# The second block's attention in head pairs, with its input normalised once and its work shifted between engines

## The chip, the cores and the metric

The kernel runs on one core of a Trainium2 chip. A core has TensorE (PE, matmuls), VectorE (DVE), ScalarE (ACT), GpSimd (POOL) and SyncE (SP), which here only issues the loads. Each engine runs its own instructions in the order written and waits on semaphores for the others. The metric is device time in microseconds (us) of one launch; lower is better.

## What is computed

A transformer block (`first_block`) and then a second one on 512 tokens of width 1024. The change lies in the second block, cut here to what matters:

```python
def second_block(x, mem, ...):
    h = rms_norm(x, norm_mix)
    q_a, k_a, v_a, u_b, gate_b, gate_c, g_a, g_b = jnp.split(h @ w_in, split_points, axis=-1)
    o_a = stick_breaking_attention(heads(q_a), heads(k_a), heads(v_a))   # 8 heads of 64
    y_b = gate_b * causal_depthwise_conv(gate_c * u_b, conv_w)           # 3 taps, 512 channels
    merged = sigmoid(g_a) * (o_a @ w_branch_a) + sigmoid(g_b) * (y_b @ w_branch_b)
    x = x + merged @ w_mix_out
    x = x + memory_cross_attention(rms_norm(x, ..), rms_norm(mem, ..), ...)
    ...
def stick_breaking_attention(q, k, v):      # per block of 128 queries, keys up to its end
    z = (q . k) * 64 ** -0.5
    log_fail = where(mask, log_sigmoid(-z), 0)          # mask: key < query
    log_later = reverse_cumsum(log_fail) - log_fail
    weights = where(mask, exp(log_sigmoid(z) + log_later), 0)
    return weights @ v
```

The input x of the second block is itself the output of a normalisation (the first block's last line), so two normalisations follow one another.

## The kernel before

Activations lie feature by token: `X[:, k, :]` is features 128k to 128k+127 of all 512 tokens. Every fp32 operand of a matmul is split into a high part (fp32r, rounded) and a low part (the rest), and each product is made of three matmuls: high by high, high by low, low by high. Weights come in units of 128 output features (128x1024, 512 KB): the load into `RAW`, ACT's copy to `WH` (helper `hi`, L1267), then the difference `WL` (helper `lo`, L1683). `WH` and `WL` have three slots (`NW`). The units `qb`, `kb` and `ub` (four each, 12 in all) have their `WL` made by POOL (L1647, `ON_POOL`), all others by DVE.

The program is one list of steps, written by the class `Order` and run through by every engine, each taking from it what is its own. A unit's matmuls (`gemm`: 24 of 128x512 into one of the two banks `G`) are emitted in two halves of 12, and each half begins with a `tick`. A step of attention is put some ticks ahead with `later(n, ...)`; steps put without it follow at once. So the list sets what stands between two halves on PE, and in what order DVE and ACT come to their work.

`block_b` is the part changed. It runs so:
- `v_gemm("vb", ...)`: the values of all heads, 96 matmuls into the banks `SC` and `TP`, from `XGh`, `XGl`, which hold x times its gain, not yet normalised. Within it `norm2` makes both row scales on DVE and ACT: `RB1` for the first block's final norm, then `RB` for the second block's, each with an Ln, an Exp and three steps on DVE (`refine`), and at last `RB` times `RB1` (L1768).
- For each head pair p the units `qb`, `kb`, `ub`, `gc`, `gb`. As `XG` isn't normalised, each result is multiplied by `RB` when it leaves PSUM: `qk_b` on DVE (L2005), then ACT's high and DVE's low part; `conv_u` on DVE, a product on POOL in `conv_g` (L1667), one more product in `taps`.
- The attention, head by head, four steps each (i, the block of 128 queries; keys 128(i+1)). `scores_b`: three matmuls of 64 rows into one of three banks (`score_bank`), then DVE adds the mask to the last 128 columns (L2050). `weights_b`: ACT's sigmoid of -z and of z (L1540, L1543), DVE's reverse running product (L2058) and the product of both (L2061). `turn_b`: PE transposes the weights by 128x128 (L1143), ACT and DVE make the two parts `WTh`, `WTl`. `pv_b`: 12 matmuls with the values into `O`. ACT and DVE take it out.
- The gates `sa`, `sb`: DVE multiplies by `RB` (`gate_b`, L2078), ACT takes the sigmoid (L1556, `sigmoid_b`), then the branches `bb`, `ba` are multiplied in (`branch`, L2085) and summed.

The first block's attention (`scores_a` and what follows it) already takes its two score maps of a head in the two halves of the rows, in alternation, six matmuls a step.

Of the kernel before, what the change touches and what calls it, by code (L numbers as in the profile page):

```python
# [11 lines left out]
ALU = mybir.AluOpType  # L12
ACT = mybir.ActivationFunctionType
# [30 lines left out]
ON_POOL = ("qb", "kb", "ub")  # L44
# [15 lines left out]
STAGES_A = (("exp_a", 1), ("weights_a", 2), ("turn_a", 4), ("wt_a", 5))  # L60
CLOSING_A = (("pv_a", 6), ("sq_a", 7), ("ss_a", 8), ("rs_a", 8), ("op_a", 9))
# [46 lines left out]
class Order:  # L108
# [80 lines left out]
    def gemm(self, name, i, step):  # L189
# [3 lines left out]
        late = wide and name in ("q", "k", "pool", "g0", "g1")  # L193
# [191 lines left out]

    def block_b(self):
        self.v_gemm("vb", 0, 4, {(0, 3): [("norm2",)], (3, 1): [("cols", "mix")]})
        for m in range(4):
            self.put("vev", "vb", 0, m)
        for k in range(8):  # L390
            self.later(2 + k, "scale_x", k)
        self.put("mask_b")
        for p in range(4):
            for w in range(2):
                self.gemm(("qb", "kb")[w], p, ("qk_b", p, w))
                self.put("qk_b", p, w)
            for j in range(8):
                h, i = 2 * p + j // 4, j % 4
                o = 1 + i + 5 * (j // 4)
                self.later(o, "scores_b", h, i)  # L400
                self.later(o + 1, "weights_b", h, i)
# [4 lines left out]
            self.put("conv_u", p)  # L406
            self.gemm("gc", p, ("conv_g", p))
            self.put("conv_g", p)
            self.later(1, "taps", p)
            self.gemm("gb", p, ("conv_y", p))  # L410
            self.put("conv_y", p)
            self.later(0, "conv_split", p)

        def gates(n):
            for w in range(2):
                self.gemm(("sa", "sb")[w], n, ("gate_b", n, w))
                self.put("gate_b", n, w)
                if n > 0:
                    self.put("sigmoid_b", n, w)

        def branch(n, w):
            self.gemm(("ba", "bb")[w], n, ("branch", n, w))
            if n == 0 and w == 1:
                self.put("sigmoid_b", 0, 0)
                self.put("sigmoid_b", 0, 1)
# [139 lines left out]
def program(nc, a, out):  # L565
# [5 lines left out]
    with ctx:  # L571
# [91 lines left out]
        def score_bank(s, n):  # L663
            return (SC[:, 0, 0:n], SC[:, 1, 0:n], M[:, 0:n])[s % 3]
# [24 lines left out]
        for v, (name, _, _) in enumerate(units):  # L689
# [6 lines left out]
        EMPTY = tally("qk", "residual", "up", "qk_b", "conv_u", "conv_g", "conv_y", "gate_b",  # L696
                      "branch", "km", "qm", "fg", "fu", "res_half")
# [3 lines left out]
        MOVED = tally("gate", "pool_in")  # L701
# [8 lines left out]

        NRM, n = {}, 0
        for step in steps:
            if step[0] in ("norm", "norm2", "norm_half"):
                n += 1 + (step[0] == "norm2")
                NRM[step] = n
# [32 lines left out]
        TURN = tally("turn_a", "turn_b")  # L748
# [1526 lines left out]
```

## Time and profile before

| | us |
|---|---|
| median of three runs | 1639.52 |
| lowest, highest | 1635.52, 1639.94 |
| the profiled execution, its time | 1636.55 |
| its span, first to last instruction | 1634.8 |
| PE busy | 1596.5 (98%) |
| DVE busy | 927.3 (57%) |
| ACT busy | 629.5 (39%) |
| POOL busy | 117.0 (7%) |

The span has 7352 matmuls. The second block's `vb` begins near 727 us of the span, its attention runs from 768 to about 946, the gates go on to about 1045. A busy PE in this profile includes the tail of each pipelined matmul (a 128x512 one is shown with 0.39 us, but the next starts 0.227 us later), so idle time of PE and the distance between starts say more than its share of busy time.

### The profile page before, as it was taken

The numbers are of one execution on the slowest core, as the hardware profiler recorded it, in microseconds if no ns is written. First come the engines' busy times: TensorE is split into PE (matmuls) and PEld (weight loads), VectorE is DVE, ScalarE is ACT, GpSimd is POOL, SyncE is SP. The second block draws the span as 40 slices with busy tenths as digits, with TensorE's granted clock in tenths as the row PEclk, the third lists the DMA queues.
The fourth block names the chain that finished last, engine by engine and source line by source line (L and its number), as shares of the span: only waits on it lengthen the run. The fifth ranks groups of instructions, "written<-read, shape, count | busy, mean of one in ns | idle before, by whom it ended". The sixth has DMA issues, their size and how long they took to land.

```text
span 1634.8 us, 19078 instructions
## 1 busy us (share of the span) xinstructions
PE 1596.5 (98%) x7352; PEld 1303.1 (80%) x7352; DVE 927.3 (57%) x1380; ACT 629.5 (39%) x1008; POOL 117.0 (7%) x82
## 2 busy tenths in 40 slices
PE   8999989999999999999999999999999999999997
PEld 6777767788888888887777787789888888888886
DVE  6767666756644545356777645555555544434435
ACT  5355665743322222263344334335444332222213
POOL 3000000010000000042221010010002000000002
PEclk9999999999999999999999999999999999999999
DMA  5243222243333323222211132335222323232322
GB/s 198 80 117 101 77 75 66 68 155 96 98 103 91 103 91 103 91 91 91 66 64 59 55 119 78 115 95 178 65 90 91 103 91 99 95 103 90 102 85 72
DMA packets 49674, 155.64 MB, mean 95 GB/s; under 512 B 6192, under 2 KB 9136, under 8 KB 49456
## 3 DMA queue, kind: packets, MB, share of 16 engines
q1 hardware_dynamic: 49584, 154.42, 30.5%
q8 instruction: 59, 0.97, 0.3%
q14 instruction: 31, 0.25, 0.1%
HBM read 148.11 MB, written 2.10 MB: 92 GB/s over the span
## 4 chain that ended last, share of the span: by engine, by line
PE 88%; DVE 6%; ACT 3%; issue 2%; DMA 0%; DVEq 0%; SPq 0%; ACTq 0%
PE G L872 77%; PE SC L872 4%; PE O L872 2%; PE TP L872 2%; DVE WL L1683 1%; PE M L872 1%; PE TP L1143 1%; ACT WH L1267 1%; DVE XGl L1684 1%; PE M L1163 0%; ACT XGh L1267 0%; ACT X L1267 0%; DVE X L2189 0%; DVE X L1971 0%; ACT T L1454 0%
## 5 line engine op out<-in xcount | busy, mean ns | idle before, releaser
L872 PE MATMUL G<-XGh,WH 128*128 128x512 f32 x1248 | 502.0, 402 | 3.1 <-DVE Vl L1684 2.2
L872 PE MATMUL G<-XGh,WL 128*128 128x512 f32 x1248 | 488.9, 392 | 0.0
L872 PE MATMUL G<-XGl,WH 128*128 128x512 f32 x1248 | 488.9, 392 | 0.0
L1683 DVE TENSOR_TENSOR WL<-RAW,WH 128x1024 fp32r<-128x1024 f32 (+3 forms) x269 | 324.0, 1205 | 143.8 <-ACT WH L1267 143.3
L1267 ACT ACTIVATE WH<-RAW 128x1024 fp32r<-128x1024 f32 (+3 forms) x281 | 283.3, 1010 | 179.6 <-PE G L872 168.7
L872 PEld LDWEIGHTS G<-XGh,WH 128*128 128x128 f32 x1248 | 235.6, 189 | 65.2 <-issue 9.3
L872 PEld LDWEIGHTS G<-XGh,WL 128*128 128x128 f32 x1248 | 235.6, 189 | 50.6
L872 PEld LDWEIGHTS G<-XGl,WH 128*128 128x128 f32 x1248 | 235.7, 189 | 48.2 <-issue 2.2
L872 PE MATMUL G<-MGh,WH 128*128 128x512 f32 x412 | 161.1, 391 | 1.8 <-DVE F L2078 1.1
L872 PE MATMUL G<-MGl,WH 128*128 128x512 f32 x412 | 160.5, 390 | 0.2 <-DVE MGl L1683 0.2
L872 PE MATMUL G<-MGh,WL 128*128 128x512 f32 x412 | 160.4, 389 | 0.0
L1971 DVE TENSOR_TENSOR X<-X,G 128x512 f32<-128x512 f32 x76 | 52.1, 686 | 142.6 <-PE G L872 142.5
L1655 POOL TENSOR_TENSOR F<-F 128x512 f32<-128x512 f32 x34 | 48.6, 1429 | 758.7 <-ACT F L1339 757.9
L872 PEld LDWEIGHTS G<-MGh,WH 128*128 128x128 f32 x412 | 77.3, 188 | 19.6 <-DVE F L2078 1.8
L872 PEld LDWEIGHTS G<-MGl,WH 128*128 128x128 f32 x412 | 77.4, 188 | 16.2 <-DVE MGl L1683 0.5
L872 PEld LDWEIGHTS G<-MGh,WL 128*128 128x128 f32 x412 | 77.3, 188 | 16.2
L872 PE MATMUL G<-Vl,WH 128*128 128x512 f32 x224 | 87.2, 389 | 0.0
L872 PE MATMUL G<-Vh,WH 128*128 128x512 f32 x224 | 87.2, 389 | 0.0
L872 PE MATMUL G<-Vh,WL 128*128 128x512 f32 x224 | 87.2, 389 | 0.0
L1267 ACT ACTIVATE MGh<-T 128x512 fp32r<-128x512 f32 x38 | 24.0, 632 | 143.3 <-DVE T L2170 63.0
L1683 DVE TENSOR_TENSOR WTl<-TP,WTh 128x128 fp32r<-128x128 f32 (+1 forms) x64 | 31.1, 486 | 57.0 <-ACT WTh L1267 56.8
L1267 ACT ACTIVATE Vh<-T 128x512 fp32r<-128x512 f32 x24 | 15.2, 632 | 101.5 <-DVE T L1984 63.7
(310 smaller groups left out, 1873.3 us busy)
## 6 DMA issues: line engine op xcount, KB each, us to landing
RAW<-in_up SPq DMA_DIRECT2D x32, 512.0 KB, 3.6
RAW<-in_dn SPq DMA_DIRECT2D x32, 512.0 KB, 3.6
RAW<-in_fg SPq DMA_DIRECT2D x22, 512.0 KB, 3.6
RAW<-in_fu SPq DMA_DIRECT2D x22, 512.0 KB, 3.6
RAW<-in_g SPq DMA_DIRECT2D x16, 512.0 KB, 3.6
RAW<-in_f SPq DMA_DIRECT2D x16, 512.0 KB, 3.5
X<-in_x SPq DMA_DIRECT2D x16, 256.0 KB, 4.6
RAW<-in_q SPq DMA_DIRECT2D x8, 512.0 KB, 3.6
```

Of the source, the lines that this page charges most:

```text
L872: return e.matmul(dst, st, mv, start=start, stop=stop, skip_group_check=True)
L1143: t = e.transpose(TP[:, i % 2, j * P:(j + 1) * P], src[:, j * P:(j + 1) * P], ID[:, :])
L1267: return e.activation(dst, src, ACT.Copy, scale=scale)
L1655: e.tensor_tensor(acc, acc, sqs[arg[1] % 2], ALU.add).then_inc(acc_done, 1)
L1683: return e.tensor_tensor(dst, src, hi.bitcast(F32), ALU.subtract)
L1684: return e.scalar_tensor_tensor(dst, src, scale, hi.bitcast(F32), ALU.mult, ALU.subtract)
L1971: e.tensor_tensor(X[:, n, :], X[:, n, :], G[:, turn_of[step] % 2, :], ALU.add).then_inc(g_empty, 1)
```

## The change

- **Normalised once.** `xsplit 2` now writes `MGh`, `MGl` (x times gain, for `vb` alone). `norm2` makes only the combined scale `RB`, from both sums at once; eight new steps `xn_mul` and `xn_lo` write `XGh`, `XGl` from `F = X * gain * RB`, between the matmuls of `vb`. `RB1` is made later (`norm2b`). The products with `RB` behind each matmul fall away: `qk_b` is ACT's high part and DVE's low part straight from PSUM, `conv_u` is a copy on ACT, the gates are one sigmoid on ACT from PSUM (`sigmoid_b` is gone), POOL's product in `conv_g` and the last one of `taps` are gone.
- **Heads in pairs.** A step of the attention is now (p, i): the scores of both heads of pair p, six matmuls in alternation between rows 0 to 63 (into `SC` bank 0) and rows 64 to 127 (bank 1). Mask, sigmoids and the product of the weights take both heads in one instruction of double width; running products, transposes and value matmuls stay one per head. The second head's turned weights lie in `QK[:, :, 4:8, :]`, its output in bank `M`.
- **Ticks.** `attention_b` places the 16 steps 2.5 ticks apart, and the parts of each at 0 (`scores_b`), 1 (`fail_b`), 2 (`weights_b`), 4 (`turn_b`), 5 (`wt_b`), then 6 (`pv_b`) and 7 (`out_b`). What leaves `G` follows one tick later instead of at once. For `qb` to `gb` and the gates one weight split moves to the second half (`late`).
- **POOL.** `ON_POOL` is empty: the 12 splits go to DVE.

```diff
-ON_POOL = ("qb", "kb", "ub")
+ON_POOL = ()
+STAGES_B = (("fail_b", 1), ("weights_b", 2), ("turn_b", 4), ("wt_b", 5))
+CLOSING_B = (("pv_b", 6), ("out_b", 7))
+PACE_B = 2.5
...
-        late = wide and name in ("q", "k", "pool", "g0", "g1")
+        late = wide and name in ("q", "k", "pool", "g0", "g1", "qb", "kb", "ub", "gc", "gb", "sa", "sb")
...
+    def attention_b(self, start):
+
+        for s in range(16):
+            p, i = s // 4, s % 4
+            o = start + int(s * PACE_B) - self.clock
+            self.later(o, "scores_b", p, i)
+            for kind, n in STAGES_B:
+                self.later(o + n, kind, p, i)
+            if i == 3:
+                for kind, n in CLOSING_B:
+                    self.later(o + n, kind, p)
+
     def block_b(self):
-        self.v_gemm("vb", 0, 4, {(0, 3): [("norm2",)], (3, 1): [("cols", "mix")]})
+        between = {(0, 3): [("norm2",)]}
+        for k in range(9):
+            at = between.setdefault((1 + k // 4, k % 4), [])
+            if k < 8:
+                at.append(("xn_mul", k))
+            if k > 0:
+                at.append(("xn_lo", k - 1))
+        between[2, 3].append(("cols", "mix"))
+        self.v_gemm("vb", 0, 4, between)
...
+        self.later(4, "norm2b")
         for k in range(8):
-            self.later(2 + k, "scale_x", k)
+            self.later(8 + 3 * k, "scale_x", k)
         self.put("mask_b")
         for p in range(4):
             for w in range(2):
                 self.gemm(("qb", "kb")[w], p, ("qk_b", p, w))
-                self.put("qk_b", p, w)
-            for j in range(8):
-                h, i = 2 * p + j // 4, j % 4
-                o = 1 + i + 5 * (j // 4)
-                self.later(o, "scores_b", h, i)
-                self.later(o + 1, "weights_b", h, i)
-                self.later(o + 3, "turn_b", h, i)
-                if i == 3:
-                    self.later(o + 6, "pv_b", h)
+                self.later(0, "qk_b", p, w)
+            if p == 0:
+                self.attention_b(self.clock + 2)
...
PE, scores_b
+                    for part in range(3):
+                        for c in range(2):
+                            r = slice(c * HEAD, (c + 1) * HEAD)
+                            q, k = ((QKh, QKh), (QKh, QKl), (QKl, QKh))[part]
+                            if part == 0 and s == 0:
+                                e.wait_ge(v_lo, VEV["vev", "vb", 0, c])
+                            elif part == 0:
+                                e.wait_ge(sb_win, s)
+                            t = mm(SC[:, c, 0:n], q[r, sq_, qs], k[r, sk_, 0:n], start=(part == 0), stop=(part == 2))
+                            if part == 2:
+                                t.then_inc(sb_done, 1)
...
ACT, fail_b
+                    e.wait_ge(sb_masked, s + 1)
+                    e.activation(T[:, 4:6, 0:n], SC[:, :, 0:n], ACT.Sigmoid, scale=-1.0).then_inc(sb_fail, 1)
+                    if s >= 2:
+                        e.wait_ge(tb_done, 2 * s - 2)
+                    e.activation(weight_pair(s, n), SC[:, :, 0:n], ACT.Sigmoid).then_inc(sb_win, 1)
...
ACT, gate_b
+                    e.wait_ge(unit_done, gemm_done(step))
+                    e.activation(sgb[n % 2][w], G[:, turn_of[step] % 2, :], ACT.Sigmoid).then_inc(g_moved, 1)
...
DVE, xn_mul and xn_lo
+                    e.scalar_tensor_tensor(F[:, k % 2, :], X[:, k, :], gain(G_MIX, k), RB[:, :], ALU.mult,
+                                           ALU.mult).then_inc(xn_mul, 1)
+                    lo(XGl[:, k, :], F[:, k % 2, :], XGh[:, k, :]).then_inc(xn_lo, 1)
```

How the order moves, at three places. First PE, where the second head pair's first scores stand (`M` and `SC` are score banks, `TP` takes transposes, `G` the units' results). Before:

```order
L872 MATMUL G<-XGh,WL 128x512
L1143 MATMUL TP<-ID,T 128x128 x3
L872 MATMUL M<-QK 128x128 x3
L872 MATMUL G<-XGh,WH 128x512
L872 MATMUL G<-XGl,WH 128x512
```

And in the changed kernel:

```order
L891 MATMUL G<-XGh,WH 128x512
L891 MATMUL G<-XGl,WH 128x512
L891 MATMUL G<-XGh,WL 128x512
L891 MATMUL SC<-QK 128x128 x6
L891 MATMUL G<-XGh,WH 128x512
L891 MATMUL G<-XGl,WH 128x512
```

Three matmuls of one head have become six of two heads. They stood one half of `ub` (12 matmuls) behind the unit `kb` whose result they read; they stand a whole `ub` (24) behind it now.

Second DVE, from the first step of `norm2` on, within `vb` (`WL` is the split of its last unit). Before:

```order
L1757 TENSOR_SCALAR T<-M 128x512
L1692 TENSOR_TENSOR T<-F 128x512
L1694 SCALAR_TENSOR_TENSOR T<-T 128x512
L1696 SCALAR_TENSOR_TENSOR F<-T,F 128x512
L1760 TENSOR_TENSOR T<-F 128x512
L1763 SCALAR_TENSOR_TENSOR T<-O,T 128x512
L1765 TENSOR_SCALAR T<-T 128x512
L1692 TENSOR_TENSOR T<-RB 128x512
L1694 SCALAR_TENSOR_TENSOR T<-T 128x512
L1696 SCALAR_TENSOR_TENSOR RB<-T,RB 128x512
L1768 TENSOR_TENSOR RB<-RB,F 128x512
L1683 TENSOR_TENSOR WL<-RAW,WH 128x1024
```

And in the changed kernel:

```order
L1826 TENSOR_SCALAR T<-M 128x512
L1829 SCALAR_TENSOR_TENSOR T<-O,T 128x512
L1748 TENSOR_TENSOR T<-RB 128x512
L1750 SCALAR_TENSOR_TENSOR T<-T 128x512
L1752 SCALAR_TENSOR_TENSOR RB<-T,RB 128x512
L1739 TENSOR_TENSOR WL<-RAW,WH 128x1024
L1799 SCALAR_TENSOR_TENSOR F<-X,GN,RB 128x512 x2
L1739 TENSOR_TENSOR XGl<-F,XGh 128x512
```

Eleven instructions ahead of the split have become five, and behind it now come the 16 that write the normalised input.

Third DVE in the midst of the attention, at the scores of 384 and 512 keys. Before (third head):

```order
L2058 SCALAR_TENSOR_TENSOR T<-T 128x384
L2061 TENSOR_TENSOR T<-T 128x383
L2050 TENSOR_TENSOR SC<-SC,MSK 128x128
L2005 SCALAR_TENSOR_TENSOR T<-G,RB 128x512
L1683 TENSOR_TENSOR QK<-T,QK 128x512
L1683 TENSOR_TENSOR MGl<-O,MGh 64x512
L1683 TENSOR_TENSOR WTl<-TP,WTh 128x2x128
L2058 SCALAR_TENSOR_TENSOR T<-T 128x512
L2061 TENSOR_TENSOR T<-T 128x511
L1683 TENSOR_TENSOR WL<-RAW,WH 128x1024
```

And in the changed kernel (second pair):

```order
L2113 SCALAR_TENSOR_TENSOR T<-T 128x384 x2
L2116 TENSOR_TENSOR T<-T 128x2x383
L2104 TENSOR_TENSOR SC<-SC,MSK 128x2x128
L1739 TENSOR_TENSOR WL<-RAW,WH 128x1024
L1739 TENSOR_TENSOR QK<-G,QK 128x512
L2113 SCALAR_TENSOR_TENSOR T<-T 128x512 x2
L2116 TENSOR_TENSOR T<-T 128x2x511
L1739 TENSOR_TENSOR WL<-RAW,WH 128x1024
```

The running products come in twos, mask and product at double width; the split that POOL made stands among them, and the step that scaled a result by `RB` ahead of its split is gone.

## Rows read from the trace of the kernel before

**Rows 1.** The page: busy time of each engine and its share

```profile
PE 1596.5 (98%) x7352; PEld 1303.1 (80%) x7352; DVE 927.3 (57%) x1380; ACT 629.5 (39%) x1008; POOL 117.0 (7%) x82
```

**Rows 2.** Windows: from:to, length, PE, PEld, DVE, ACT, POOL busy, clock, DMA share, GB/s

```profile
768.00:931.00 163.00, 159.16 (x734) 123.14 (x734) 116.00 (x188) 64.01 (x134) 27.69 (x13) 1.00 0.20 60
934.00:937.00 3.00, 2.69 (x12) 2.26 (x13) 3.00 (x6) 1.46 (x3) 0.00 (x0) 0.78 0.13 36
937.00:940.00 3.00, 3.00 (x10) 2.38 (x9) 0.56 (x1) 0.00 (x0) 0.00 (x0) 0.65 0.57 181
```

**Rows 3.** Waits of PE, 727 to 1030 us: us in total, times, longest

```profile
PE TP L1143 <- DVE T L2061: 2.7, 1, 2.7
PE SC L872 <- DVE QK L1683: 2.6, 2, 1.3
PE SC L872 <- DVE WL L1683: 2.0, 1, 2.0
PE M L872 <- DVE QK L1683: 1.3, 1, 1.3
PE G L872 <- DVE F L2078: 1.1, 1, 1.1
```

**Rows 4.** Timeline of PE, first head: start, us, what; six rows

```profile
767.82 0.39 PE L872 MATMUL G<-XGh,WL 128*128 128x512 f32 x1
768.14 0.55 PE L872 MATMUL SC<-QK 64*128 64x128 f32 x3
768.62 0.50 PE L872 MATMUL G<-XGh,WH 128*128 128x512 f32 x1
...
771.55 0.61 PE L872 MATMUL SC<-QK 64*128 64x256 f32 x3
...
775.04 0.78 PE L872 MATMUL M<-QK 64*128 64x384 f32 x3
...
778.81 0.97 PE L872 MATMUL SC<-QK 64*128 64x512 f32 x3
```

**Rows 5.** Timeline of PE, the first block's attention, score steps

```profile
102.44 0.55 PE L872 MATMUL SC<-QK 64*128 64x128 f32 x6
...
112.12 0.79 PE L872 MATMUL SC<-QK 64*128 64x384 f32 x6
...
118.88 0.96 PE L872 MATMUL SC<-QK 64*128 64x512 f32 x6
```

**Rows 6.** Timeline of PE, scores that begin a head pair, with the idle time before

```profile
807.60 0.52 PE L872 MATMUL M<-QK 64*128 64x128 f32 x3 [1.26 <-DVE QK L1683]
...
849.30 0.52 PE L872 MATMUL SC<-QK 64*128 64x128 f32 x3 [1.29 <-DVE QK L1683]
```

**Rows 7.** Timeline of DVE in `norm2`, within `vb`

```profile
734.48 0.68 DVE L1757 TENSOR_SCALAR T<-M 128x512 f32<-128x512 f32 x1
...
744.19 2.77 DVE L1768 TENSOR_TENSOR RB<-RB,F 128x512 f32<-128x512 f32 x1
746.88 1.21 DVE L1683 TENSOR_TENSOR WL<-RAW,WH 128x1024 fp32r<-128x1024 f32 x1
```

**Rows 8.** Groups by form, DVE, 20 to 60 us: xcount, busy us, mean ns, idle

```profile
L1729 DVE SCALAR_TENSOR_TENSOR X<-X,GN,RB 128x512 f32<-128x512 f32 x8 | 5.9, 746 | 0.0
```

**Rows 9.** Groups by form, DVE, 734 to 1045 us

```profile
L1683 DVE TENSOR_TENSOR WL<-RAW,WH 128x1024 fp32r<-128x1024 f32 x26 | 31.7, 1219 | 8.7 <-ACT WH L1267 8.7
L2058 DVE TENSOR_TENSOR_SCAN T<-T 128x512 f32<-128x512 f32 x8 | 11.0, 1370 | 0.0
...
L2005 DVE SCALAR_TENSOR_TENSOR T<-G,RB 128x512 f32<-128x512 f32 x8 | 5.5, 683 | 5.1 <-PE G L872 5.1
```

**Rows 10.** Timeline of POOL, then of DVE, one moment near 773 us

```profile
772.85 2.62 POOL L1647 TENSOR_TENSOR WL<-RAW,WH 128x1024 fp32r<-128x1024 f32 x1 [14.10 <-ACT WH L1267]
...
773.32 2.30 DVE L2061 TENSOR_TENSOR T<-T 128x127 f32<-128x127 f32 x1
```

**Rows 11.** Groups by form, ACT, 734 to 1045 us

```profile
L1540 ACT ACTIVATE T<-SC 128x512 f32<-128x512 f32 x6 | 3.5, 590 | 1.1 <-DVE SC L2050 1.1
```

More of the change, by code:

```diff
@@ L714, in program @@
                 n += 1 + (step[0] == "norm2")
-                NRM[step] = n
+                SUM[step] = n
         ln_done, r_sq = sem("ln_done"), sem("r_sq")
@@ new lines, in _ @@
+                    for part in range(3):
+                        for c in range(2):
+                            r = slice(c * HEAD, (c + 1) * HEAD)
[7 more added lines that the diff above has]
+                                t.then_inc(sb_done, 1)
+                elif kind == "turn_b":
+                    p, i = arg
+                    s, n = 4 * p + i, (i + 1) * P
+                    e.wait_ge(wb_done, s + 1)
+                    for c in range(2):
+                        if s == 0:
+                            e.wait_ge(v_lo, VEV["vev", "vb", 0, 2 + c])
+                        else:
+                            e.wait_ge(wtb_lo, 2 * s - 1 + c)
+                        for j in range(i + 1):
+                            t = e.transpose(TP[:, c, j * P:(j + 1) * P], weight_pair(s, n)[:, c, j * P:(j + 1) * P],
+                                            ID[:, :])
+                        t.then_inc(tb_done, 1)
+                elif kind == "pv_b":
+                    p = arg[0]
+                    for c, bank in enumerate((O, M)):
+                        if p > 0:
+                            e.wait_ge(ob_lo, 2 * p - 1 + c)
+                        elif c == 0:
+                            e.wait_ge(v_lo, VEV["vev", "vb", 0, 3])
+                            e.wait_ge(ms_done, NRM["norm2",])
+                        else:
+                            e.wait_ge(col_done, COL["cols", "mix"])
+                        e.wait_ge(wtb_lo, 8 * p + 7 + c)
+                        pv_heads(bank, turned_of(c), lambda j: j, p).then_inc(pvb_done, 1)
@@ new lines, in _ @@
+                    if s >= 2:
+                        e.wait_ge(tb_done, 2 * s - 2)
+                    e.activation(weight_pair(s, n), SC[:, :, 0:n], ACT.Sigmoid).then_inc(sb_win, 1)
+                elif kind == "wt_b":
+                    p, i = arg
+                    s, n = 4 * p + i, i + 1
+                    for c in range(2):
+                        if i == 0 and p > 0:
+                            e.wait_ge(pvb_done, 2 * p - 1 + c)
+                        e.wait_ge(tb_done, 2 * s + 1 + c)
+                        v = TP[:, c, 0:n * P].rearrange("p (j q) -> p j q", q=P)
+                        hi(turned_of(c)[0][:, 0:n, i * P:(i + 1) * P], v).then_inc(wtb_hi, 1)
+                elif kind == "out_b":
+                    p = arg[0]
+                    for c, bank in enumerate((O, M)):
+                        r = slice(c * HEAD, (c + 1) * HEAD)
+                        e.wait_ge(pvb_done, 2 * p + 1 + c)
+                        hi(MGh[r, p, :], bank[r, :]).then_inc(ob_hi, 1)
+                elif kind == "gate_b":
@@ L2057, in _ @@
+                    W_, fail = weight_pair(s, n), T[:, 4:6, 0:n]
                     e.wait_ge(sb_fail, s + 1)
-                    e.tensor_tensor_scan(back, back, back, 1.0, ALU.mult, ALU.min).then_inc(wb_all, 1)
-                    e.wait_ge(wb_all, s + 1)
+                    for c in range(2):
+                        back = T[:, 4 + c, 0:n][:, ::-1]
+                        e.tensor_tensor_scan(back, back, back, 1.0, ALU.mult, ALU.min).then_inc(wb_all, 1)
+                    e.wait_ge(wb_all, 2 * s + 2)
```

331 lines of the change are left out of this document (148 added, 183 removed).

## The prediction

> **What bounds the kernel now.** I read the page first: TensorE is busy for 98% of the span, VectorE for 57%, ScalarE for 39%, GpSimd for 7% [rows 1]. So the kernel is as long as PE's list, and a change pays only by shortening that list or by taking away an idle moment of PE. The windows say the same of the part that is changed: from 768 to 931 us PE is busy 159.2 of 163 us and DVE 116.0 [rows 2]. Then the waits of PE from 727 to 1030 us, which name each idle moment: 2.7 us for the last head's weights, 2.6 and 1.3 us for a split of q or k, 2.0 us for a weight split within `vb`, 1.1 us for a result that a gate had not yet freed, 9.7 us in all [rows 3]; two more of 0.4 us I leave out of account. Last the timeline of PE itself, for what its list costs between two units.
>
> **The scores in pairs.** In the second block one head's step is three matmuls of 64 rows. They take 0.55, 0.61, 0.78 and 0.97 us for the four key lengths, and the next unit's first matmul starts 0.07 us before such a row ends (768.14 plus 0.55, against 768.62) [rows 4]. That is 2.91 less 4 times 0.07, or 2.63 us a head. Each visit also costs at its edges: 768.14 comes 0.32 us after the last matmul of the unit instead of 0.227, and the first one behind lasts 0.50 instead of 0.39 us [rows 4], 0.2 us a visit, 0.8 a head. One head's scores: 3.4 us. In the first block, where a step holds six matmuls in alternation between the two halves of the rows, it takes 0.55, 0.79 and 0.96 us at three of these lengths [rows 5], the same for twice the work. The change makes 16 steps of six out of 32 of three, with the same shapes, so four heads' worth goes: 4 times 3.4 = **13.7 us**. Transposes (80) and value matmuls (96) stay as many and as long, 0.
>
> **The waits for q and k.** Each head pair's first scores come 12 matmuls behind `kb`, and its result goes DVE, ACT, DVE; PE idles 1.26 and 1.29 us for it [rows 6], three times in all, 3.9 us by rows 3. Now ACT reads PSUM at once, DVE follows, and 24 matmuls (5.4 us) lie between. One result's path is then some 0.63 and 0.69 us: it fits four times. **3.9 us** go, and what is late next is only the order of the tick, below.
>
> **The last head.** 2.7 us [rows 3]: its weights had little left to hide them, one unit and a half. Behind it the granted clock was 0.78 and 0.65 for 3 us each [rows 2], that is 0.22 and 0.35 of 3 us, 1.7 us more; PE had stood for 2.7 us ahead of it. In the changed kernel the last pair's scores, at 284 ticks, and its transposes, at 288, have two halves of `sb` and `sa` and the 12 matmuls of `bb` between them, 3 times 2.7 and some 1.8 us of scores and transposes, 9.9 us. The path: scores 0.97 [rows 4], two running products 2.7 [rows 9], and by the width of the rows of 512 mask 0.4, sigmoid 1.05, product 1.2, together 6.3 us, with five hops and a split in between about 8.3. **4.4 us** go, with 1.6 us to spare.
>
> **Within `vb`.** DVE is in `norm2` from 734.48 to 746.96 us, its last step at 2.77 us, and PE is 2.0 us idle for the split that ends at 748.09 [rows 3, 7]. Eleven instructions become five: 0.68, 0.7, then 1.3 on ACT, then three of 0.7, so `RB` stands at 739.3 and the split at 740.5, for a unit that PE takes up at about 746. **2.0 us** go. But the unnormalised input is no longer what `qb` reads. Eight times DVE now makes a product of 0.75 us [rows 8] and a difference of 0.69: 11.5 us, with two splits of 1.22 [rows 9] 14.1 us, from 740.5 to 754.7. PE ends `vb` at 752.4 (754.4 before, less 2.0) and wants slice k of the first unit 0.68 us times k later: the last one at 757.2. So 2.5 us to spare; covered, at nothing. If that cover were gone it costs what DVE is late, once.
>
> **The gates.** Sixteen products by `RB` of 0.69 us leave DVE, and ACT reads PSUM itself. The 1.1 us of rows 3 goes, but ACT's read now stands behind a step of the memory's split that waits for DVE; by the same sums that is up to 0.5 us. **0.6 us** go.
>
> **DVE, which gets more to do in less time.** The way from one head pair to the next was 849.30 less 807.60 = 41.7 us [rows 6]. Less 1.3 of waiting and 3.4 for the scores it is 36.9. In 163 us DVE works 116.0 [rows 2]. Coming: 9 of the 12 splits at 1.22 us [rows 9], 11 us. Going: six products of 0.68 us for q and k [rows 9], four each for `conv_u` and `taps`, 9.6 us in all; the masks and weight products in half as many instructions, some 4 us. Four more of the `scale_x` fall into this stretch, 2.8 us. That leaves 116 for what took 163 us and will take 144 (163 times 36.9 by 41.7), 81%. And a part of the 116 wasn't work: a product of 127 columns took 2.30 us from 773.32, just while POOL's split ran from 772.85 to 775.47, and `norm2`'s last step took 2.77 for 0.7 [rows 7, 10]. POOL keeps no split, so such rows should be short, and DVE's share nearer 76%. The Trainium skill, page "SBUF — State Buffer", section "SBUF: two separate sides", calls this an exclusive lock that the loser waits out; the row agrees, and by that rule each of the 12 splits could have held DVE up once.
>
> Tick by tick the fullest stretch is `weights_b` of 384 columns to that of 512, three ticks. DVE has 5.3 us (turned parts 0.8, running products 1.9, product 1.0, mask 0.4, split 1.2), then 0.7 (k's low part), then 4.9 (2.5, 1.2, 1.2), against PE's 3.8, 2.7 and 3.4 (a half of 2.7 each, with scores or transposes), so it ends 1 us behind, 1.7 with a `scale_x`. What PE next needs from it, the transposes two ticks on, is 6 us away. A new wait isn't seen, but not every hop is in this sum. The first block, with the same pattern, makes PE wait there. Between 0 and 6 us I take **2.0 us** of new waits, nearest to what the sum shows.
>
> **The sum.** 13.7 + 3.9 + 4.4 + 2.0 + 0.6 - 2.0 = 22.6 us, and with the smaller waits that I left out about 23. The profiled execution took 1636.55 us, so 1613.5. It lies 3.0 us below the median of the three runs (1639.52), near the lower end of their spread; a median of the changed kernel could thus read up to 3 us more. I take one of it: **1614.5 us**.
>
> **The rivals.**
>
> *Waits come back (0.16).* DVE is at 76 to 81% here, and in-order work behind a full engine comes late: say 1 to 3 us for each of the four pairs, with the 5 us edges of `vb` lost too. For it: DVE's two sources of cover, `kb` and the weights, are the ones PE already waited on. Against: the ticks are longer than the paths. 1614.5 + 4 to 12: 1618 to 1626.
>
> *The pair's banks (0.04).* The three score banks become one pair, so the next scores wait for both sigmoids. A sigmoid of 512 columns takes 0.59 us [rows 11], one of 1024 about 1.05. From scores to free banks: 0.97 + 0.4 + 2.1 + hops, 3.8 us by these widths, once in 2 or 3 ticks of 3.7 us. Decisive once ACT is over 3 us late with the first sigmoid; then 1 us in each of 16 steps: 1630. The Trainium skill, page "TensorEngine Tiling (Array Packing)", section "Performance Considerations", warns of just this, that reading PSUM may become the bottleneck once TensorE is faster by tiles. No row of the trace before has this double-width form.
>
> *The pairs don't overlap (0.03).* If the second head's matmuls wait for something the first's don't, 13.7 us stay: 1628. The list has them in one piece of six and both wait for the same count, so hardly.
>
> *Slower than before (0.03).* DVE becomes the bound through its hops. Within a pair it has some 22 places where it waits for PE or ACT. Its work is 28 of 36.9 us, so up to 0.40 us of idle time at each is free. A hop in which ACT makes the high part costs DVE 0.7 us when nothing else is queued. If all 22 did, DVE would need 43.4 us a pair, 6.5 too many, or 26 in four, against 22.6 gained: 1640 to 1645. It decides from about 0.66 us a hop. Against it: most hops now have another tick's work queued in them, which is what the ticks do.
>
> **How the numbers follow.** Forecast 0.74, the rivals 0.16, 0.04, 0.03 and 0.03. The forecast's own bounds: all waits gone and none new, 1610.5, less 2 for what I left out; six new ones and the median's 3, 1620. To hold 8 in 10 the range must reach into the first rival: 1608 to 1621. About 0.3% (5 us) is what a measurement of this kernel can tell from no change. All but the last rival lie below 1634.6: faster 0.95, within 0.3% 0.02, slower 0.03.
>
> **What would show it.** Scores in rows of x6 at 0.55 to 0.97 us; no wait of PE at the pairs' first scores; 36.9 to 38 us from one pair to the next; PE's waits from 727 to 1030 us under 3 us in all; a clock of 1.00 from 930 us on; the value-side `SC` matmuls without the wait; DVE's short products all near 0.3 us, none above 2; DVE busy 76 to 81% from the first scores to the last. It is wrong if PE waits for `SC` on ACT (the banks), for `XG` at the first `qb` (the normalised input), or for DVE's weights in each pair.

## The result, and the profile after

| | before | changed |
|---|---|---|
| median of the runs | 1639.73 us (4 runs, 1635.52 to 1640.84) | 1611.13 us (4 runs, 1608.91 to 1613.0) |
| ratio | | 0.983, 95% interval 0.9807 to 0.9853 |
| profiled execution, its span | 1636.55, 1634.8 us | 1608.91, 1607.0 us |
| mean granted clock of the profiled execution | 0.994 | 0.997 |

The forecast was 1614.5 us, in a range from 1608 to 1621. The four executions of the changed kernel lie in two groups: clock 0.997 with spans of 1607.0 and 1607.9 us, clock 0.993 with 1611.1 and 1610.6. The profiled one is of the first group. Where an experiment differs by less than 4 us, the medians alone don't decide. As all these kernels have equally many matmuls on PE, I then compare the start of the same matmul in the two traces, once ahead of the changed part (near 724 us) and once behind it (near 1021 us): what is gained or lost between the two belongs to the edit. One of the twelve executions of the kernel before without GpSimd's splits, below, took 1776.88 us at a mean clock of 0.85 and is left out.

The page of the changed kernel, busy time of each engine, to hold against [rows 1]:

```profile
PE 1577.4 (98%) x7352; PEld 1293.1 (80%) x7352; DVE 911.4 (57%) x1342; ACT 634.2 (39%) x988; POOL 80.6 (5%) x66
```

Both kernels have 7352 matmuls, and PE's busy time is 19.1 us shorter. No matmul left PE's list; more of them overlap, and there are fewer waits and less time at the low clock. Now PE's waits from 727 to 1030 us, all of them:

```profile
PE TP L1212 <- DVE WTl L1739: 1.4, 1, 1.4
PE G L891 <- ACT F L1617: 0.3, 1, 0.3
```

Of [rows 3] nothing is left, and one wait is new: 1.4 us ahead of the last pair's last transposes. The timeline of PE gives the scores, over one pair and the first step of the next:

```profile
798.73 0.55 PE L891 MATMUL SC<-QK 64*128 64x128 f32 x6
...
805.77 0.62 PE L891 MATMUL SC<-QK 64*128 64x256 f32 x6
...
818.83 0.79 PE L891 MATMUL SC<-QK 64*128 64x384 f32 x6
...
825.71 0.96 PE L891 MATMUL SC<-QK 64*128 64x512 f32 x6
...
835.67 0.55 PE L891 MATMUL SC<-QK 64*128 64x128 f32 x6
```

Six matmuls last as long as three did in [rows 4], and from pair to pair it is 835.67 less 798.73, 36.94 us (41.7 before, 36.9 forecast).

The window over the attention (length, then PE, PEld, DVE, ACT, POOL busy, the granted clock, DMA share, GB/s):

```profile
766.00:917.00 151.00, 149.57 (x754) 119.17 (x753) 107.19 (x159) 69.48 (x114) 0.00 (x0) 1.00 0.23 70
```

DVE is busy for 107.19 of 151 us, 71%, where I forecast 76 to 81. The clock stays at 1.00, also behind the new wait of 1.4 us, which ends at 911.06; before it fell to 0.78 and 0.65 behind the wait of 2.7 us [rows 2].

**Where the 27.8 us of span went.** Both lists have equally many matmuls, so I compare the start of the n-th one in both. Before `norm2` the changed kernel is 2.1 us ahead (VectorE's first row of `norm2` starts at 732.39 instead of 734.48, [rows 7]), though nothing is changed there. The clock did that. Windows of before, then of the changed kernel:

```profile
56.00:60.00 4.00, 3.02 (x10) 2.48 (x11) 4.00 (x6) 1.65 (x3) 0.00 (x0) 0.81 0.45 135
...
236.00:240.00 4.00, 4.00 (x12) 3.08 (x11) 4.00 (x8) 2.05 (x6) 1.62 (x1) 0.58 0.00 0
```

```profile
56.00:60.00 4.00, 2.97 (x13) 2.48 (x14) 4.00 (x6) 1.71 (x3) 0.00 (x0) 1.00 0.44 135
...
232.00:236.00 4.00, 3.13 (x11) 2.52 (x12) 4.00 (x15) 2.69 (x8) 0.00 (x0) 0.60 0.00 0
236.00:240.00 4.00, 4.00 (x21) 3.29 (x20) 3.93 (x7) 2.64 (x5) 1.65 (x1) 0.97 0.03 7
```

The low stretch near 59 us is missing in the changed kernel, and the one from 232 us ends some 3 us earlier. The executions of one kernel differ in the same way. The first experiment below changes nothing ahead of 727 us; its profiled execution (clock 0.993) is 4.1 us behind the changed kernel's (0.997) at the same matmul near 724 us, and 4.2 us behind near 1021 us. One of its low stretches, then the same time in the changed kernel:

```profile
184.00:187.00 3.00, 3.00 (x8) 2.34 (x7) 3.00 (x9) 2.24 (x6) 0.00 (x0) 0.50 0.00 0
```

```profile
184.00:187.00 3.00, 3.00 (x17) 2.48 (x16) 2.93 (x7) 3.00 (x8) 0.00 (x0) 1.00 0.00 0
```

In both the stretch follows the same wait of PE for VectorE, 1.45 us long.

The other terms, in the order of the prediction:

| term | forecast | measured |
|---|---|---|
| scores in pairs | 13.7 | 13.8 |
| waits for q and k | 3.9 | 3.9 |
| last head: wait, clock behind it | 2.7 + 1.7 | 1.3 (2.7 went, 1.4 came) + 1.6 |
| within `vb` | 2.0 | 2.3 |
| gates | 0.6 | 2.4 |
| new waits elsewhere | -2.0 | 0 |
| clock ahead of the changed part | none | 2.1 |
| not assigned | | 0.4 |

### The profile page after: what moved, and what is told of

It reads as the page before. It is cut to its first block, busy times and chain, and to the rows that moved or that the text cites. A ratio compares the mean times of both kernels' runs of the same rounds, so it can differ in the third digit from the quotient of the medians.

```text
span 1607.0 us, 18953 instructions
## 1 busy us (share of the span) xinstructions
PE 1577.4 (98%) x7352; PEld 1293.1 (80%) x7352; DVE 911.4 (57%) x1342; ACT 634.2 (39%) x988; POOL 80.6 (5%) x66
## 4 chain that ended last, share of the span: by engine, by line
PE 93%; DVE 4%; ACT 2%; issue 1%; DMA 0%; SPq 0%; DVEq 0%; ACTq 0%
PE G L891 81%; PE SC L891 4%; PE TP L891 2%; PE O L891 2%; PE M L891 1%; DVE WL L1739 1%; ACT WH L1300 1%; PE TP L1212 1%; PE TP L1160 0%; PE M L1180 0%; DVE X L2244 0%; ACT T L1496 0%; DVE X L1785 0%; ACT L1297 0%; DVE XGl L1739 0%
## 5 line engine op out<-in xcount | busy, mean ns | idle before, releaser
L1739 DVE TENSOR_TENSOR WL<-RAW,WH 128x1024 fp32r<-128x1024 f32 (+3 forms) x281 | 338.6, 1206 | 183.1 <-ACT WH L1300 182.6
L891 PEld LDWEIGHTS G<-Vh,WH 128*128 128x128 f32 x224 | 42.0, 188 | 8.7
```

The lines of the kernel that those rows point to most:

```text
L891: return e.matmul(dst, st, mv, start=start, stop=stop, skip_group_check=True)
L1739: return e.tensor_tensor(dst, src, hi.bitcast(F32), ALU.subtract)
```

## The experiments

### Do the two halves of the rows really overlap?

The term of 13.7 us has two parts that the result does not tell apart: two heads side by side, and 16 visits to the scores instead of 32. The first run takes the alternation away and does one head's three matmuls, then the other's.

```diff
-                    for part in range(3):
-                        for c in range(2):
+                    for c in range(2):
+                        for part in range(3):
```

> The changed kernel with one thing undone: in each scores_b step the six matmuls stand head by head (rows 0 to 63 three times, then rows 64 to 127 three times), no longer in alternation. Same count, same banks, same waits. Pairing theory (13.7 us of the gain is the overlap of the two halves of the rows): the six take 1.0 to 1.9 us instead of 0.55 to 0.96, the way from one head pair to the next grows from 36.9 to about 39.6 us (less than 3.4, as the visits stay 16 and their edges aren't paid twice), span 10 to 11 us longer, 1618 us of span. Rival (the gain came from waits and ticks, the overlap is small): under 4 us longer. If DVE were the bound, nothing is lost, 0 us.

Measured: 1613.34 us (1613.0 to 1613.56), ratio 0.9852 (0.9837 to 0.9866). Its spans at clock 0.993 and 0.994, 1611.1 to 1611.7, are about those of the changed kernel at 0.993, 1610.6 and 1611.1, and between the same two matmuls it loses 0.1 us (4.12 and 4.22 us behind). So no cost. Its timeline of PE has the step of 512 columns at

```profile
903.82 0.97 PE L891 MATMUL SC<-QK 64*128 64x512 f32 x6
```

and the rows of that tile in the 0.02 us from 903.82 (durations in ns, minimum, median, maximum; first and last start) are

```profile
L891 PE MATMUL SC<-QK x2: 493/493/493, 903.8 to 903.8; 64*128 64x512 f32 x2
```

Two of the six start together, in this order too. They must be of different halves, since on one half (next run) they start 0.23 us apart. What I expected of the alternation fell: what the program says between the halves matters little, as long as the six stand together. That leaves open whether it is the overlap that saves the time. So the next run puts both heads on the same half:

```diff
-  t = mm(SC[:, c, 0:n], q[r, sq_, qs], k[r, sk_, 0:n], start=(part == 0), stop=(part == 2))
+  t = mm(SC[:, c, 0:n], q[0:HEAD, sq_, qs], k[0:HEAD, sk_, 0:n], start=(part == 0), stop=(part == 2))
```

> The changed kernel, but in the second attention both heads of a pair read q and k from rows 0 to 63 of the array, so the second head computes the scores of the first again. Same instructions, same order, same waits. If the two halves really work side by side (the theory: the six products of 512 columns take 0.96 us because head 1's start beside head 0's, which the trace of the run with the heads in turn shows within 0.01 us), then every visit grows by three products: 3 x 128, 256, 384 and 512 columns at 2.4 GHz are 0.16, 0.32, 0.48 and 0.64 us, 1.6 us a pair, 6.4 us in all, and the time is 1611 + 6.4 = about 1617.5. The other 7.4 of the 13.8 us then came from going to the scores 16 times rather than 32. Rival 1, the gain is in the fewer visits alone: no change, 1611. Rival 2, the gain is in the overlap alone: 13.8 us, about 1625.

The text on record speaks of the second attention alone, but the same line stands in the first attention, and the edit is made at both places: 16 steps in the second and 32 in the first. Measured: 1632.77 us (1630.45 to 1633.36), 21.6 us above the changed kernel. The steps, on PE's timeline:

```profile
853.76 0.88 PE L891 MATMUL SC<-QK 64*128 64x128 f32 x6
...
861.14 0.97 PE L891 MATMUL SC<-QK 64*128 64x256 f32 x6
...
874.51 1.32 PE L891 MATMUL SC<-QK 64*128 64x384 f32 x6
...
881.92 1.66 PE L891 MATMUL SC<-QK 64*128 64x512 f32 x6
```

Against 0.55, 0.62, 0.79 and 0.96 that is 0.33, 0.35, 0.53 and 0.70 us more, 1.91 a pair: 7.6 us in the second attention's four and 15.3 in the first's eight. Of the latter 1.3 are hidden, since PE's waits there for `SM` fell from 7.9 to 6.6 us.

7.6 + 15.3 - 1.3 = 21.6. So both rivals fall: of the 13.8 us, 7.6 are overlap. The other 6.2 are what is left for the 16 visits fewer, 0.39 each. The starts of single matmuls bear that out: around a step of 512 columns the first score starts 0.32 us behind the last matmul of the unit instead of 0.227, each head's first and last score matmul take 0.33 and 0.32 us to the next start instead of 0.23, and the first matmul behind takes 0.33 instead of 0.23, some 0.4 us in all. The Trainium skill, page "TensorEngine Tiling (Array Packing)", section "Tiling Modes", says that tiles load weights and multiply in parallel, and that changing the mode drains the array. The first agrees with these rows; the second would explain the edges of a visit, but no run here separates it. My expectation of 6.4 was low because it counted columns: three matmuls of 128 columns cost 0.33 us more, 0.11 each, where 128 columns at 2.4 GHz are 0.053. The same page of the Trainium skill, section "Performance Considerations", puts a floor of some 60 cycles under a matmul; the one seen here in the short steps lies higher.

### GpSimd's splits, in both kernels

The kernel before, with all of its splits on VectorE (`ON_POOL = ()`), and the changed kernel with twelve of them given back (`ON_POOL = ("qb", "kb", "ub")`).

> The kernel before with one part of the change alone: the 12 splits on DVE instead of POOL. Theory: the 2.0 us wait in vb goes or shrinks (the step of 2.77 us falls to 0.7), the three waits for q and k stay (their way is through DVE, ACT, DVE), and DVE has 12 splits more but loses the held-up instructions: 0 to 3 us faster. Rival (without POOL's help DVE is late in the old order, where all evacuations are on it): 3 to 10 us slower, more waits of PE for DVE.

Measured: 1636.09 us (1631.54 to 1637.3, eleven executions), ratio 0.9987 (0.9974 to 0.9999); profiled span 1632.3 at clock 0.994, against 1634.8 at 0.994. Of PE's waits only the one of 2.0 us within `vb` is gone. VectorE's step of `norm2` that took 2.77 us [rows 7] is

```profile
743.56 0.69 DVE L1768 TENSOR_TENSOR RB<-RB,F 128x512 f32<-128x512 f32 x1
```

and the product of 127 columns (2.30 us, [rows 10]) is

```profile
770.65 0.29 DVE L2061 TENSOR_TENSOR T<-T 128x127 f32<-128x127 f32 x1
```

So a split on GpSimd did hold VectorE up. Over the attention it sums up: from 766 to 929 us VectorE is busy for 113.87 us with nine splits (11 us) more in its list than the 116.0 us of before [rows 2], so some 13 of those 116.0 us were not work. And the wait within `vb`, which I had laid to the eleven steps of `norm2`, goes with GpSimd's split alone, with all eleven still there. The next run has GpSimd's splits and the shorter `norm2`, and no such wait: either edit of the change would have been enough.

> The changed kernel with the 12 weight splits of qb, kb and ub back on POOL. Theory (DVE has room, it is busy 107 of 151 us in the attention, and PE waits for nothing there): no change beyond 2 us; DVE's work falls by 12 times 1.22 us but some of its short products take 1.6 to 2.7 us again, so that DVE is busy about as long. Rival A (taking POOL away was needed: a DVE held up comes late for PE): 3 to 8 us slower, with waits of PE for DVE. Rival B (DVE was near its limit and POOL's help would be welcome): 1 to 2 us faster.

Measured: 1610.19 us (1609.71 to 1612.44), ratio 0.9836 (0.982 to 0.9851): no difference that I can measure (less than 0.1 us between the same two matmuls), and PE's waits are the same two rows. VectorE is held up again, by form, mean in ns (the changed kernel has 681 and 677):

```profile
L1739 DVE TENSOR_TENSOR MGl<-F,MGh 128x512 fp32r<-128x512 f32 x4 | 7.3, 1827 | 0.0
L2113 DVE TENSOR_TENSOR_SCAN T<-T 128x256 f32<-128x256 f32 x8 | 7.3, 949 | 0.1
```

That is 4.6 and 2.2 us, and nothing that PE needs is late for it. Taking the splits from GpSimd brought the changed kernel no time; it was worth some 2 us in the kernel before, at one place. The Trainium skill, page "SBUF — State Buffer", section "SBUF: two separate sides", has the exclusive lock; these rows agree with it. Its price hangs on where the held-up row stands.

### The input normalised once: how near was the other end?

`norm2b` is moved from four ticks later to right behind `norm2`:

```diff
-        between = {(0, 3): [("norm2",)]}
+        between = {(0, 3): [("norm2",), ("norm2b",)]}
...
-        self.later(4, "norm2b")
```

> The changed kernel with norm2b (the scale RB1 that only the residual needs) made right behind norm2 within vb, ahead of the eight steps that write the normalised input. It puts 3.9 us (0.7, two ACT steps, three of 0.7) between them. My sum for vb: DVE then ends the low parts at about 158.6 minus the start of the count instead of 154.7 (3.9 us later), PE wants the last at 157.2 on the same count, so PE waits 1 to 1.5 us in the first unit qb, in total less than 2 us. The split of vb's last unit comes 3.9 us later too, 5 us of cover, no wait. Rival (the cover is larger than I summed): no wait at all, 0 us. Rival (the chain is on the path from the start): 3.9 us.

Measured: 1615.54 us (1614.54 to 1616.25), ratio 0.986 (0.9843 to 0.9876), 4.4 us above the changed kernel. PE now waits for the input's low parts, and the clock pays again (windows from 756 us; the wait on PE's timeline):

```profile
758.92 0.50 PE L890 MATMUL G<-XGl,WH 128*128 128x512 f32 x1 [1.91 <-DVE XGl L1738]
```

```profile
756.00:759.00 3.00, 1.04 (x4) 0.56 (x4) 2.03 (x4) 3.00 (x5) 0.00 (x0) 1.00 0.00 0
759.00:762.00 3.00, 3.00 (x8) 2.38 (x9) 3.00 (x5) 2.35 (x5) 0.00 (x0) 0.57 0.73 219
762.00:765.00 3.00, 3.00 (x13) 2.38 (x12) 2.36 (x3) 0.45 (x1) 0.00 (x0) 0.86 0.62 175
```

Waits of 2.3 us (1.91 and 0.42), and low clock of 0.43 and 0.14 of 3 us, 1.7 us: 4.0 together. A wait is counted from the end of the row before, 0.16 us behind where the next matmul would have started, and the matmul behind it takes 0.1 us longer, so two waits cost 0.5 more; between the same two matmuls the run loses 4.6 us. How much room did the changed kernel have? Its last low part, and PE's first read of it, are

```profile
753.23 0.68 DVE L1739 TENSOR_TENSOR XGl<-F,XGh 128x512 fp32r<-128x512 f32 x1
...
755.09 0.39 PE L891 MATMUL G<-XGl,WH 128*128 128x512 f32 x1
```

The low part is done at 753.91, 1.2 us ahead of PE, where the prediction had 2.5. In this run it is done at 758.86 (758.18 and 0.68), and PE would have read it at 756.05, 2.8 us earlier. PE itself came 1.0 us later than in the changed kernel, from ahead of the edit; 4.95 us later for VectorE less 1.0 is 4.0, the 1.2 and the 2.8.

### Is VectorE near to being the bound?

Twenty splits of weights are done twice on VectorE, with a wait between:

```diff
+                    if units[v][0] in ("qb", "kb", "ub", "gc", "gb"):
+                        lo(wl, RAW[:, v % NRAW, 0:c], wh).then_inc(twice, 1)
```

> The changed kernel with each of the 20 weight splits of qb, kb, ub, gc and gb done twice by DVE (the same values again), 20 times about 1.3 us. In the attention DVE would be busy some 133 of 151 us, 88%. It measures how much room DVE has, which my slower rival put at 0.40 us for each of 22 hops, 9 us a pair. Theory (DVE has room for 6 us a pair): under 6 us longer, with a few waits of 0.5 to 2 us at the fullest ticks. Rival (DVE is already nearly the bound through its in-order waits): 4 times 4 us and more, 16 to 26 us longer.

Measured: 1614.1 us (1612.55 to 1615.72), ratio 0.9852 (0.9835 to 0.9868), about 3 us more (3.3 between the same two matmuls). The window of the attention, and PE's waits but for the gate's 0.3:

```profile
766.00:917.00 151.00, 148.25 (x746) 117.60 (x745) 128.57 (x179) 68.98 (x115) 0.00 (x0) 1.00 0.22 70
```

```profile
PE TP L1213 <- DVE WTl L1740: 1.9, 3, 1.4
PE G L892 <- DVE XGl L1740: 1.3, 1, 1.3
PE SC L892 <- issue: 0.8, 1, 0.8
```

With VectorE at 128.57 of 151 us, 85%, the way from the second pair to the third is 37.38 us (first scores at 801.55 and 838.93), 0.4 more than in the changed kernel; the next way is 0.4 longer too, the first not at all. Most of the loss stands ahead of the first pair: the two waits of 1.3 and 0.8 us, 2.5 us with what stands at their edges. The clock did not fall. The rival in which VectorE becomes the bound was far off: 21 us of extra work in this window cost some 3.

### The place in ticks

Four kernels move something by a tick: the whole attention earlier (`self.clock + 1`) or later (`+ 3`, from `+ 2`), the last step's turning, splitting and value product later, or the last step's `weights_b` earlier.

> The changed kernel with the whole attention one tick earlier: each pair's first scores stand 12 matmuls behind kb, as they did before the change, not 24. It tells apart what took away the 1.3 us at each pair: the distance, or the shorter way out of PSUM (ACT, DVE instead of DVE, ACT, DVE). Theory: the way is now 1.4 us and starts at once, 2.7 us of cover, so no wait comes back from q and k; as all steps change place against splits and evacuations, up to 2 us elsewhere. Rival (the distance did it): 3 waits of 0.5 to 1.3 us for the low part of k or q, 2 to 4 us longer.

Measured: 1616.66 us (1614.77 to 1617.28), ratio 0.9865 (0.9848 to 0.9882), 5.5 us more by the medians and 4.1 us between the same two matmuls. PE's waits:

```profile
PE SC L891 <- issue: 4.0, 4, 1.5
PE TP L1212 <- DVE WTl L1739: 1.0, 1, 1.0
```

The four (0.39, 1.47, 1.32 and 0.86 us) stand ahead of the first scores of the four pairs. "Issue" means that the profile names no releaser; I take it from the times. Around the largest the timeline reads

```profile
801.45 0.68 DVE L1739 TENSOR_TENSOR QK<-G,QK 128x512 fp32r<-128x512 f32 x1
...
802.24 0.55 PE L891 MATMUL SC<-QK 64*128 64x128 f32 x6 [1.47 <-issue]
```

VectorE makes the low part of k from 801.45 to 802.13, and PE goes on 0.1 us later. These are the waits for q and k of [rows 6], back at the old price. The shorter way out of PSUM alone did not take them away; the tick did. But the tick does two things. It puts 12 more matmuls ahead of the scores, and it changes the place of k's low part in VectorE's list. In the changed kernel it stands ahead of the running products of 512 columns:

```profile
793.33 0.69 DVE L1739 TENSOR_TENSOR QK<-G,QK 128x512 fp32r<-128x512 f32 x1 [0.92 <-ACT QK L1300]
793.94 2.33 DVE L2113 TENSOR_TENSOR_SCAN T<-T 128x512 f32<-128x512 f32 x2
```

A tick earlier these and the product behind them stand first, 3.5 us from 797.94, although ACT has k's high part ready at 797.99. The low part right behind ACT would have been done near 798.7, and PE stood idle only from 800.77. So by this sum 12 matmuls were distance enough, as I had expected, and the place in VectorE's list was what made k late. No run moves the one without the other.

> The changed kernel with the whole second attention one tick later, the other way to the run with it a tick earlier, which brought four waits of 1.0 to 1.5 us ahead of the scores back. The theory: in the changed kernel the q and k of a pair are ready less than a tick ahead of its scores and nothing waits, so a tick more buys nothing there; and it puts the last step's work a tick further into the gates, where the waits that the change took away (2.4 us in the kernel before) or that for the narrow unit (1.4) come back or go. Theory A (the gates' waits were gone because the attention ends earlier): +0.5 to +2.5 us, waits of the gates named in the trace. Theory B (they were gone because the steps are split into hops): the same within 1 us, with the wait of 1.4 us gone, so 1610 to 1611.

Measured: 1611.12 us (1607.56 to 1613.35), ratio 0.9839 (0.9821 to 0.9857). PE's waits, all:

```profile
PE G L891 <- ACT F L1617: 0.3, 1, 0.3
```

The wait of 1.4 us is gone and the gates' waits have not come back: theory B. Its span is 1605.7 us at clock 0.997, where the changed kernel has 1607.0 and 1607.9; between the same two matmuls it gains 1.6 us (0.3 behind, then 1.4 ahead).

The new wait itself, on the timeline of the changed kernel:

```profile
902.29 1.02 ACT L1588 ACTIVATE T<-SC 128x1024 f32<-128x1024 f32 x1
...
903.54 0.60 ACT L1617 ACTIVATE T<-G 128x512 f32<-128x512 f32 x1 [0.24 <-PE G L891]
...
904.04 1.05 ACT L1300 ACTIVATE WH<-RAW 128x1024 fp32r<-128x1024 f32 x1
...
905.12 1.23 DVE L1739 TENSOR_TENSOR WL<-RAW,WH 128x1024 fp32r<-128x1024 f32 x1 [2.73 <-ACT WH L1300]
...
906.26 2.33 DVE L2113 TENSOR_TENSOR_SCAN T<-T 128x512 f32<-128x512 f32 x2
908.63 1.22 DVE L2116 TENSOR_TENSOR T<-T 128x1022 f32<-128x1022 f32 x1
909.77 0.68 DVE L2140 TENSOR_TENSOR T<-T,G 128x512 f32<-128x512 f32 x1
910.37 0.55 DVE L1739 TENSOR_TENSOR WTl<-TP,WTh 128x384 fp32r<-128x384 f32 x1
...
911.06 1.07 PE L1212 MATMUL TP<-ID,T 128*128 128x128 f32 x8 [1.43 <-DVE WTl L1739]
```

ACT's sigmoids of the last scores start the chain. Then ACT takes a gate's sigmoid from PSUM, for which PE has to finish a unit, and only then the high part of a weight slice. VectorE is 2.73 us idle for that split, while the running products behind it in its list could have begun. Everything that follows is late. PE could have begun at 909.63 (911.06 less 1.43). The weights that it has to turn are finished at 909.85, 0.2 us late. But `TP` must be free as well, and the low part that frees its first half, that of the step before (384 columns), stands behind the product of a gate's branch (L2140) and ends at 910.92. That is the row which the wait names. If this reading holds, `weights_b` ahead of the split must take the wait away, and so must more room behind:

```diff
-                self.later(o + n, kind, p, i)
+                self.later(o + n - ((s, kind) == (15, "weights_b")), kind, p, i)
```

> The changed kernel with weights_b of the last step one tick earlier, so that on DVE it stands ahead of the split of sb, not behind it. In the trace of the changed kernel DVE stood idle from 902.4 to 905.1 us for that split, whose copy on ACT stood behind the sigmoid of a gate that waited for its matmuls. Theory A (it is this in-order wait that makes DVE late, not the distance in ticks): DVE begins the running products near 902.4, the wait of 1.4 us goes with the transposes where they are. Theory B (the ticks are too short there for the path turn, ACT, DVE, turn): the wait stays at 0.5 us or more.

Measured: 1610.4 us (1607.12 to 1611.54), ratio 0.9827 (0.981 to 0.9845); only the wait of 0.3 us is left. At the last scores its profiled execution is 3.9 us behind the changed kernel's, from far ahead of the edit. VectorE's running products are at

```profile
906.31 2.34 DVE L2113 TENSOR_TENSOR_SCAN T<-T 128x512 f32<-128x512 f32 x2
```

which is 902.4 on the changed kernel's count instead of 906.26, as theory A says, and the split of `sb` now comes behind them, at 909.82. The low part that frees `TP` starts at 911.55, 907.7 on that count instead of 910.37. Its spans are 1605.2 and 1606.2 at clock 0.997.

> The changed kernel with the very last attention step (pair 3, 512 keys) from its transposes on one tick later. The one wait of PE that is left in the attention, 1.4 us for DVE's low part of the transposed weights ahead of this step's transposes, stands where a tick holds only the 12 matmuls of a narrow unit. Theory: the wait goes, span 1.4 us shorter, nothing new (the value matmuls still end 2.7 us ahead of the unit that reads them). Rival: the delay moves on to the value matmuls or to ba, 0 us, with a wait there.

Measured: 1611.29 us (1610.64 to 1612.78), ratio 0.9841 (0.9826 to 0.9856); the wait is gone here too, with spans of 1608.8 to 1610.9 at clock 0.994.

So three edits remove the wait. Between the same two matmuls each is 1.6 us shorter than the changed kernel: the whole attention later goes from 0.3 us behind to 1.4 ahead, `weights_b` from 3.9 to 2.3 behind, the last step's turning from 4.1 to 2.5 behind. The medians, 1611.12, 1610.4 and 1611.29 against 1611.13, don't show that, since the executions fall on different clocks. The edit of `weights_b` has the lowest median, but nothing here ranks the three.

## Why the prediction was right, and where its steps were not

The time and the reason held: PE's list was the bound, and most of what shortened it is what I had priced. The sum came closer than its steps. New waits (2.0 us too many), the gates (1.8 too few) and the last head (1.5 too many gained) were off, and the last two cancel in part; that is luck. The lower bound of the forecast is also misadded: without new waits its own terms give 1611.5, not 1610.5.

**Scores in pairs.** 13.8 us for 13.7. The price was taken from steps of six in the first block, the same form at the same place in the list, and that made it good. Its parts are now known: 7.6 of overlap and, as the rest, 6.2 of visits. The rival "the pairs don't overlap" was therefore priced wrongly: it had all 13.7 us stay, but without overlap the visits would still have become fewer, and the time would have been about 1619 (1611.1 + 7.6), not 1628.

**Waits for q and k.** 3.9 us as said, and the tick does it, as the run a tick earlier shows (4.0 us back). The prediction gave the shorter path and the greater distance as reasons. The rows point at a third, that k's low part no longer stands behind running products in VectorE's list.

**The last head.** This step failed in part. I added up the path of the last scores alone (8.3 us against 9.9) and found 1.6 us to spare. In the trace that path takes 10.25 us (899.60 to 909.85), as a split and a gate's sigmoid stand ahead of the running products, and a second condition ends later still, at 910.92: the bank `TP`, which the step before had to leave. PE waits 1.4 us. What stood in line in front of the path, and the bank, were left out. The clock's share, 1.7, held at 1.6.

**Within `vb`.** 2.3 us for 2.0. Behind it 1.2 us were to spare, not 2.5: PE came when the sum said, VectorE 1.3 us later, as its two splits there each wait 1.0 us for ACT's high part. The run with both norms first shows that this cover was really used up. The reason for the 2.0 was only half right: the run of before without GpSimd's splits loses the wait with `norm2` unchanged.

**The gates.** 0.6 forecast, 2.4 measured. I priced one wait of 1.1 us and took off 0.5 for a new one, which came with 0.3. The two of 0.4 us that I left aside went too; they ended with the branch's product (L2085), which has to follow the gate's sigmoid. Each of the three cost 0.27 us more between starts than its idle time says. They stay away with the attention a tick later, so an earlier end of the attention is not the cause. Whether it is the going of the product by `RB`, ACT's reading of PSUM itself, or the new places in the list wasn't separated.

**New waits.** I took 2.0 us between 0 and 6; there were none besides the last head's and the gate's 0.3. VectorE at 71% had more room than its forecast of 76 to 81 said. The sum of removed products was nearly right; what I overrated was the part of the old 116.0 us that was work: some 13 us of it were held-up rows, where the step from 81 to 76% takes off 7. And the run with twenty splits twice shows how little the share says: at 85% a pair grows by 0.4 us at most. The rival of the pair's banks did not come: a sigmoid of both heads takes 1.02 us, as estimated, and PE never waits for `SC` on ACT.

**The clock.** 2.1 us of the profiled difference lie ahead of the change, where of the low stretches of the clock in the execution of before one is missing after and one is shorter. That belongs to the execution, not to the change. Without them the profiled gain is 25.7 us, for a forecast of 23.

## What to carry to other kernels

When a stage is limited by TensorE, look for steps that use half of the rows: put two of them next to each other, on different halves, and the second is nearly free (six matmuls in 0.96 us where three took 0.97); count the visits that vanish as a gain of their own. Place a step by what stands ahead of it in every engine's list, and by the bank that it writes, not by its own path alone: one tick decided the waits for q and k, and one gate's sigmoid in front of a split made the larger new wait. Price a wait of PE with its clock behind it, which here was 1.6 us behind 2.7, 1.7 behind 2.3, and nothing in other cases. And where executions differ by more than the edit, compare the start of one and the same matmul on both sides of it.

## What the runs showed of the hardware

- Matmuls on different halves of the rows start together even when two others of the first half stand between them in the program (0.97 us for six of 512 columns in this order, 0.96 in alternation, 1.66 on one half).
- The clock after a wait: it fell behind 2.7 us of idle time (0.78, 0.65) and behind 0.42 and 1.91 us in near succession (0.57, 0.86), and stayed at 1.00 behind a single 1.4 us near 911 us and a single 1.25 us. That is no rule: behind one and the same wait of 1.45 us in the first block it was 0.50 in one execution and 1.00 in another.
- Four executions of one program differ by 4 us with the mean granted clock (0.997 and 0.993). Between two profiled executions with these clocks the whole difference (4.1 us) has arisen by 724 us, and the clock was low in stretches of one where it was not in the other.
- A split on GpSimd took 2.4 to 2.6 us in most cases and held short rows of VectorE up to about that long (0.29 us became 2.30, 0.69 became 2.77). In the kernel before one such row made PE wait for 2.0 us; in the changed kernel none did.
